# A transformer step on one Trainium2 core: the first modulation product of each layer is placed in other steps of the attention pipeline, and a bias table is loaded and prepared later

## The reference, cut to what matters

```python
def modulate(cvec, w_mod_l, b_mod_l):
    m = jnp.einsum('bd,de->be', jax.nn.silu(cvec), w_mod_l) + b_mod_l
    return jnp.split(m[:, None, :], N_MOD, axis=-1)      # sh1, sc1, g1, sh2, sc2, g2, 1024 columns each

# per layer
h = rmsnorm(x, norm1) * (1 + sc1) + sh1
p = h @ w_in                                 # queries, keys and values of three kinds of heads
# latent attention (8 heads), windowed attention with a sink (4 heads),
# 2-D neighbourhood attention (4 heads) with a learned position bias from rpb
x = x + g1 * (concat(heads) @ w_out)
h2 = rmsnorm(x, norm2) * (1 + sc2) + sh2
x = x + g2 * mixture_of_experts(h2)          # top 2 of 16 experts
```

## Time and profile before

| | us |
|---|---|
| three runs | 1337.96, 1335.44, 1338.13 |
| median | 1337.96 |
| the profiled execution, its own time | 1338.34 |
| its span, first to last instruction | 1336.3 |
| TensorE busy in it | 1279.6 (96%) |
| VectorE, ScalarE, GpSimd busy | 613.7, 358.8, 152.5 |
| mean granted clock of TensorE | 0.991 of full speed |

### The profile page before, as it was taken

How to read it: one execution, slowest core, us unless ns; L and a number is a source line. 1 busy time by engine, 2 the same in 40 slices (tenths; PEclk the granted TensorE clock), 3 DMA queues, 4 the chain that set the end, 5 groups by cost and what they waited for, 6 DMA issues and landing times. The chain is left out here.

```text
span 1336.3 us, 17216 instructions
## 1 busy us (share of the span) xinstructions
PE 1279.6 (96%) x6042; PEld 735.3 (55%) x6042; DVE 613.7 (46%) x1519; ACT 358.8 (27%) x931; POOL 152.5 (11%) x257
## 2 busy tenths in 40 slices
PE   6999999999999999999999999989999999999997
PEld 3555555565666564444455555566666656444443
DVE  0132266444566463433343224655556536344438
ACT  1121255434343210000012114563444311100001
POOL 2210220000000110000142003000000011000014
PEclk9999999998999999999999999999899999999999
DMA  9976996499111489999694038430201139999966
GB/s 355 363 248 220 347 332 254 162 359 327 42 64 64 168 333 398 361 374 367 260 334 161 16 140 291 151 128 15 88 33 64 63 130 352 404 368 360 362 270 246
DMA packets 125441, 313.16 MB, mean 234 GB/s; under 512 B 9882, under 2 KB 58426, under 8 KB 112688
## 3 DMA queue, kind: packets, MB, share of 16 engines
q1 hardware_dynamic: 90896, 243.13, 49.8%
q0 software_dynamic: 12848, 45.39, 9.0%
q10 hardware_dynamic: 21616, 23.60, 5.3%
HBM read 232.14 MB, written 80.71 MB: 234 GB/s over the span
## 5 line engine op out<-in xcount | busy, mean ns | idle before, releaser
L790 PE MATMUL ps<-ring,big 128*128 128x384 f32 (+2 forms) x640 | 230.7, 520 | 1.7 <-DVE big L1773 1.3
L790 PEld LDWEIGHTS ps<-ring,big 128*128 128x128 f32 x640 | 120.3, 190 | 104.6 <-issue 63.7
L871 PE MATMUL ps<-ring,arena 128*128 128x512 f32 x384 | 169.3, 594 | 1.9 <-ACT arena L1406 1.9
L502 PEld LDWEIGHTS ps<-consts,arena 128*128 128x128 f32 (+2 forms) x880 | 103.7, 143 | 79.1 <-issue 50.9
L502 PE MATMUL ps<-consts,arena 128*128 128x128 f32 (+2 forms) x880 | 129.7, 278 | 15.7 <-ACT arena L1227 6.6
L711 PE MATMUL ps<-ring,big 128*128 128x512 f32 x320 | 143.0, 598 | 0.8
L563 PE MATMUL ps<-arena 64*128 64x128 f32 (+5 forms) x576 | 137.9, 430 | 6.1 <-DVEq L1822 3.4
L1227 ACT ACTIVATE arena<-ps 128x384 f32<-128x384 f32 (+3 forms) x140 | 69.1, 493 | 221.3 <-PE ps L502 221.3
L871 PEld LDWEIGHTS ps<-ring,arena 128*128 128x128 f32 x384 | 71.2, 190 | 83.1 <-issue 83.1
L563 PEld LDWEIGHTS ps<-arena 64*128 64x128 f32 (+1 forms) x576 | 79.4, 196 | 65.8 <-issue 57.8
L711 PEld LDWEIGHTS ps<-ring,big 128*128 128x128 f32 x320 | 59.0, 190 | 70.4 <-issue 66.4
(11 more groups left out here) (237 smaller groups left out, 1481.9 us busy)
## 6 DMA issues: line engine op xcount, KB each, us to landing
ring<-in_w_mod SPq DMA_DIRECT2D x40, 1024.0 KB, 11.8
ring<-in_w_up SPq DMA_DIRECT2D x22, 1024.0 KB, 9.7
ring<-in_w_gate SPq DMA_DIRECT2D x22, 1024.0 KB, 7.6
slots<-zeros ACTq DMA_DIRECT2D x8, 2560.0 KB, 14.4
slots<-zeros SPq DMA_DIRECT2D x8, 2560.0 KB, 20.2
arena<-in_w_down SPq DMA_DIRECT2D x16, 1024.0 KB, 12.7
arena<-slots SPq DMA_DIRECT2D x30, 512.0 KB, 6.4
slots<-arena POOLq DMA_DIRECT2D x30, 512.0 KB, 9.6
```

The source lines that it names most:

```text
L502: return pe.transpose(out, in_, ident)
L790: mm = pe.matmul(ps[:, c, 0:CHUNKS[c][1]], hT[:, s, k, :], slot[c][:, k, 0:CHUNKS[c][1]], start=(k == 0), stop=(k == KD - 1))
L871: mm = pe.matmul(ps[:, b, :], xgT[:, b, k * P:(k + 1) * P], w_gu[q][:, :, k, :], start=(k == 0), stop=(k == KD - 1))
```

## The change

The constant `MOD_AT` becomes a list of two steps for each group. The first group moves from steps 3 and 4 to steps 1 and 3; groups 2 and 3 keep their steps. What follows a group (bias row, turning, copying) hangs on its second step and so comes one step earlier for the first group alone: on VectorE the bias row in step 4 and the copy in step 6, on TensorE the turning in step 5. The fillers of steps 1 and 3 go, those of step 0 stay. SyncE's wait for the last transposes of the input stage goes, and the table's load moves behind the eight modulation loads. GpSimd's four additions move from p = 2 to 5 to p = 4 to 7. ScalarE computes one exponential of a single column just before phase 2.

```diff
-MOD_AT = (3, 10, 17)
+MOD_AT = ((1, 3), (10, 11), (17, 18))
...
                         if turning:
                             turn(s - 3, 0)
-                        if s == 3:
-                            spin(7, 3)
                         if s < len(pairs):
                             scores(s, (0, 1))
-                        if s < 2:
+                        if s == 0:
                             spin(7, 4)
...
                         for g, at in enumerate(MOD_AT):
-                            if s in (at, at + 1) and (g < 2 or L < DEPTH - 1):
-                                ks = range(4 * (s - at), 4 * (s - at) + 4)
+                            if s in at and (g < 2 or L < DEPTH - 1):
+                                ks = range(4 * at.index(s), 4 * at.index(s) + 4)
                                 mod_group(L + g // 2, (g + 1) % 3, ks)
                         for g in (1, 2):
-                            if s == MOD_AT[g - 1] + 3:
+                            if s == MOD_AT[g - 1][1] + 2:
                                 mod_columns2(L, g)
-                        if s == MOD_AT[2] + 3 and L < DEPTH - 1:
+                        if s == MOD_AT[2][1] + 2 and L < DEPTH - 1:
                             mod_columns(L + 1)
...
-                sp.wait_ge(T.full, T[("h", L, TILES - 1)])
-                sp.dma_start(bias, t_in["rpb"][L]).then_inc(rpb_in, 16)
                 for half in range(2):
                     sp.wait_ge(S[half].full, S[half][("in", L, TILES - 1)])
                     for part in range(2):
                         mod_load(L, 1, part, (2 * half, 2 * half + 1))
+                sp.dma_start(bias, t_in["rpb"][L]).then_inc(rpb_in, 16)
                 pass_by("sp")
...
                 meet(act, "act")
 
+                act.activation(stat["es"][:, 0:1], mhalf[:, 0:1], ACT.Exp)
                 attention(L, 2)
...
-                    if 2 <= p < 6:
-                        if p == 2:
+                    if 4 <= p < 8:
+                        if p == 4:
                             pool.wait_ge(rpb_in, 16 * (L + 1))
-                        bh = bias[:, p - 2, :].rearrange("p (j c) -> p j c", j=15)
+                        bh = bias[:, p - 4, :].rearrange("p (j c) -> p j c", j=15)
                         pool.tensor_tensor(bh, bh, mad, ALU.add).then_inc(bias_done, 1)
...
                         for g, at in enumerate(MOD_AT):
-                            if s == at + 2 and (g < 2 or L < DEPTH - 1):
+                            if s == at[1] + 1 and (g < 2 or L < DEPTH - 1):
                                 mod_rows(L + g // 2, (g + 1) % 3)
                         for g in (1, 2):
-                            if s == MOD_AT[g - 1] + 4:
+                            if s == MOD_AT[g - 1][1] + 3:
                                 mod_columns2(L, g)
-                        if s == MOD_AT[2] + 4 and L < DEPTH - 1:
+                        if s == MOD_AT[2][1] + 3 and L < DEPTH - 1:
                             mod_columns(L + 1)
```

## The result

The changed kernel took 1347.53 us (median of four, 1345.61 to 1348.16), the kernel before beside it 1336.74 us (1335.44 to 1338.13): a ratio of 1.0078, 95% interval 1.0061 to 1.0096, some 10.8 us slower. The profiled execution is the fastest of the four, 1345.61 us, 7.3 us above the profiled 1338.34 of before. The traces can therefore account for 7.3 us; the other 3.5 lie in how the executions differ among themselves. The mean granted clock of TensorE was 0.988 in the profiled one of the four and 0.987 in the other three. One execution of the kernel before, 1512.29 us at a granted clock of 0.84 beside nineteen others of 1335 to 1341, is left out of the experiments.

What follows compares the result with a forecast made beforehand. TensorE, busy 96% of the span, bounds the kernel through its serial issue and waits. Terms +2.6 - 1.4 + 4.0 = +5.2 us on the median of 1337.96 give 1343 us, range 1337.5 to 1347.5.

Steps and rivals of the forecast that it cites:

- The sum of +5.2 us: Whole kernel: +2.6 us in layer 0, -1.4 us in layer 1, +4.0 us for the additions.
- The wait for the weights: Step 1: TensorE waits 4.7 us for modulation weights in layer 0, under 1 us in layer 1.
- Layer 1: First steps of phase 2 in layer 1: scores 2 later by 2.1 us, less 3.57 in step 4: -1.4 us.
- The half group behind the gap at full clock: Step 1, layer 0: half group starts at 169.8 and takes 3.57 us; net +2.6 us in layer 0.
- rival (a): TensorE's clock falls in layer 0's 4.7 us gap: 2.4 us more, 1345.6 us; chance 0.25.
- The fillers at nothing: Step 3: scores 3 wait 0.26 us for VectorE even behind the fillers, so removing these gains nothing.
- The additions: Steps 4 to 7: GpSimd's additions lose their cover and slow VectorE's multiplications, +2.0 us a layer, +4.0 us.
- The count of two meetings a layer before: Kernel before: two of four additions meet a normalisation on VectorE, both covered by half groups in steps 3 and 4.
- rival (d): A meeting costs all that is left of an addition, up to 2.25 us instead of 1.02: 1348.1 us; chance 0.07.
- The table's load at nothing: Table's load behind the weights: 0 us for the weights; lands at 180 in layer 0, 825 in layer 1.
- The exponential and the bias row's move: Exponential takes ScalarE's 1.28 us table load out of step 0, 0 us; bias row a step earlier, 0 us.

Runs made afterwards that it cites:

- e5: Changed kernel with layer 0's zero stores given out in three steps of the input projection instead of four: 1341.27 us, ratio 1.0022 to the kernel before.
- e1: Changed kernel with nine zero matmuls ahead of the first half group in step 1 of layer 0: 1341.98 us, ratio 1.0044 to the kernel before.
- a0: Changed kernel measured once more, unaltered, on the chip of some later runs: 1348.68 us, ratio 1.0090 to the kernel before.
- e2: Changed kernel with the table's load and GpSimd's additions put back as in the kernel before: 1344.34 us, ratio 1.0048 to the kernel before.
- e8: Changed kernel with three zero matmuls put back into step 3 of both layers, in another PSUM bank: 1347.17 us, ratio 1.0072 to the kernel before.
- e12: Kernel before with only the fillers of steps 1 and 3 taken out: 1346.88 us, ratio 1.0050 to the kernel before.
- e3: Changed kernel, but layer 0 keeps its first group in steps 3 and 4 with the old fillers: 1341.04 us, ratio 1.0032 to the kernel before.
- e6: Changed kernel with zero stores ahead and table's load and additions early, without step-3 fillers: 1336.67 us, ratio 0.9996 to the kernel before.
- e9: Changed kernel with zero stores ahead, table's load and additions early, and three step-3 fillers in another bank: 1336.43 us, ratio 0.9991 to the kernel before.
- e11: e9 plus one zero matmul behind every fourth narrow matmul at the start of phase 4: 1333.14 us, ratio 0.9955 to the kernel before.
- e4: Kernel before with only the table's load and GpSimd's additions moved as in the change: 1341.88 us, ratio 1.0038 to the kernel before.

## Why the verdict held, and where the sum failed

The verdict (slower) came, and the measured 1347.53 us stands on the upper bound of the range, 1347.5. That it stands no further out is partly luck: the kernel before took 1336.74 us beside it, 1.2 us less than the 1337.96 that the range was built on. The sum of +5.2 us was half of what came. The mechanisms in it (a wait for weights, a gain in layer 1, additions without cover) were found in the trace; two effects on the clock were not in it.

**The wait for the weights: right.** 4.7 us forecast, 4.76 in the trace; under 1 us in layer 1, 0.84. e5 shows the reason: with the zero stores done a step earlier the gap is gone.

**Layer 1: right.** -1.4 us forecast, -1.14 at the scores of step 5.

**The half group behind the gap at full clock: wrong, the step that failed.** The sum let the half group start at 169.8 and take 3.57 us; it started at 169.43 and took 6.57. So +2.6 us was forecast at step 5 and +5.65 measured; 2.93 of the difference of 3.05 are the half group at the low clock. e1 is the proof: with the gap filled the half group takes 3.64 us. This is rival (a). The prediction gave it a chance of 0.25 against the forecast's 0.29, because the clock line of the kernel before was full nearly everywhere. That was no evidence: in steps 1 and 3 of that kernel fillers stood where the gaps would have been. The Trainium skill (TensorE: Matmul & The Clock Gate, section "HAM oscillation — how this bites in real kernels") makes a DMA wait between groups of matmuls the rule for a lowered clock; the four traces in which the gap stood unfilled agree: after, a0, e2 and e8 took 5.02 to 6.57 us for the half group behind it.

**The fillers at nothing: the same mistake.** "Taking these fillers away gains nothing" is true of the chain: scores 3 keep their 3.17 us behind scores 2. But I took them for idle time in disguise and asked only what their removal would gain, not what it would cost. e12 priced it in the kernel before: 6.7 us (4.1 to 9.4). In the changed kernel the four of step 1 are missed in layer 0, where they would have stood in the gap of 4.76 us; in layer 1 the half group takes their place but for 0.84 us. The three of step 3 are missed in both. In thirteen layers of the traces the gap of 1.56 us stood between the two half groups. The second one was slowed in six of them, at 4.71 to 5.34 us (layer 0 of a0, e2 and e5, layer 1 of e2, e3 and e6), and took 3.64 us in seven (both layers of after and of e1, layer 1 of a0 and e5, layer 0 of e6). With these fillers (e8, e9, e11) it took 3.64 us in six layers of six. But e8 against a0 and e6 against e9 show no difference in time, so a price of these three in the changed kernel is not shown.

**The additions: right in kind, mis-sized.** +2.0 us a layer was forecast for steps 5 to 10; 1.5 and 1.8 came, but by e2 only 0.7 and 1.0 are the additions. (The count of two meetings a layer before was one short: the addition at 165.66 met the pair of multiplications at 167.40, which took 1.02 us instead of 0.75.) Their three meetings in layer 0 lengthened the multiplications by 2.4 us together, so most of that was covered. The other 0.8 a layer goes with the half group that left step 4; that the bias row and the turning beside it are the cause was not tried. In e4, where they stand alone, the clock fell once behind the delay that they made; the kernel is 5 us slower, of which this trace shows 3.4. Of rival (d) the mechanism was right and the price too high: a multiplication does wait for the addition's end, as the meetings quoted here and in the earlier trace rows show, but it came upon an addition half done, so that a meeting cost 0.7 to 1.4 us and not 2.25. That also agrees with the Trainium skill (SBUF — State Buffer, section "SBUF: two separate sides"), and the start of the fourth addition in e4 shows the hold the other way round.

**The table's load at nothing: right for the weights, wrong for GpSimd.** It landed at 179.4 in layer 0 of the changed kernel, as forecast (180), but at 833.8 in layer 1, 17.2 us behind the first scores where 15.2 was forecast, and GpSimd waited 3.42 us for it. In e4 a wait of 8.27 us bunched the additions of layer 0. In the changed kernel everything else was later, and it did no harm that a trace shows.

**The exponential and the bias row's move: nothing shown.** The table load of 1.28 us is where it was expected (815.97 in layer 1), and no wait of the chain ends on it.

**What stays open.** The profiled executions are 7.3 us apart and the medians 10.8. The rest goes with a lower granted clock, as the table and the 72 executions show, but not with a place. The falls at the start of phase 4 lasted some 14 us in layer 0 and 7 in layer 1, in the traces of before and of after alike, but anything from 7 to 20 us in those of the other kernels, and e11, which takes them away, also takes away most of the spread. That the changed kernel has more or longer falls there than the kernel before is argued, not shown; a single trace of each kernel cannot show it. Nor did any run find what decides whether the clock falls behind a gap of 1.56 us.

## What to carry to other kernels

Before a consumer is moved ahead, read when its load lands, in every layer: the same step had 4.7 us to wait in one and 0.8 in the other. A matmul whose result nobody reads is not idle time; ask what the clock does without it, and price that as a term of the sum and not as a rival. Where a single trace does not account for a difference of medians, compare the mean granted clock of all executions. Where a kernel's times scatter by half a per cent, look for a place where the clock falls in every trace: filling it here was worth more than the whole rearrangement.

## What the runs showed of the hardware that I had not expected

The clock fell behind a gap of 2.04 us in layer 0 and one of 2.01 in layer 1 of e12, and one of 1.56 us preceded a fall in six layers of thirteen. In the stretch of 24-column matmuls TensorE is not idle at all, and in all thirteen traces without fillers there the clock falls to 1.2 GHz inside it or within some 2 us of its end, in both layers; one 256-column zero matmul for every four of them kept it at 2.4 GHz (e11), although it lengthens the stretch from 3.58 us (294.68 to 298.26) to 5.30 (293.00 to 298.30). And the clock falls are a source of scatter: the kernel with the fewest has times within 1.8 us of one another, and in the kernel before an execution at a mean granted clock of 0.987 takes some 7 us more than one at 0.993.
